# A hybrid encoder layer on one core: attention's tiles taken in another order, copies reordered, and half of the first output unit's products placed in the last head

## What is computed

```python
q = (_rms(c_q, norm_q[l]) @ w_uq[l]).reshape(B, L, N_HEADS, NOPE_DIM + ROPE_DIM)
kv = (_rms(c_kv, norm_kv[l]) @ w_ukv[l]).reshape(B, L, N_HEADS, NOPE_DIM + V_DIM)
s = (einsum('bqhd,bkhd->bhqk', q_n, k_n) + einsum('bqhr,bkr->bhqk', q_r, k_r))
p = softmax(s * scale)          # over the keys of one sequence
attn = einsum('bhqk,bkhd->bqhd', p, v).reshape(B, L, N_HEADS * V_DIM) @ w_o_attn[l]
```

## Time and profile before

| | |
|---|---|
| median of 3 runs | 1320.33 us (1320.19 to 1321.05) |
| the profiled execution's own time | 1321.35 us |
| its span | 1319.6 us |
| TensorE busy | 1281.5 us (97%), 7181 matmuls |
| VectorE busy | 689.2 us (52%) |
| ScalarE busy | 466.1 us (35%) |
| GpSimd busy | 328.7 us (25%) |
| chain that ended last | PE 87%, DVE 5%, ACT 4%, issue 3% |
| attention, 361 to 571 us | TensorE busy 195.62 of 210.00 us, VectorE 159.83, ScalarE 134.27, GpSimd 87.04 |

### The profile page before, as it was taken

The page is one execution under the profiler, slowest core; times in us unless marked ns, Lnnn a source line. Parts: engine busy times, 40 slices in busy tenths (PEclk is TensorE's granted clock), DMA queues, the critical chain, the costliest instruction groups (busy, mean ns, idle before and its releaser), DMA issues.

```text
span 1319.6 us, 18184 instructions
## 1 busy us (share of the span) xinstructions
PE 1281.5 (97%) x7181; PEld 1109.9 (84%) x7181; DVE 689.2 (52%) x781; ACT 466.1 (35%) x689; POOL 328.7 (25%) x198
## 2 busy tenths in 40 slices
PE   6999999999999999989999999999999999999996
PEld 4888888888888888878888888888888888888885
DVE  4699999998768788773732131111111233343334
ACT  6211123422266666643522242222222333333325
POOL 2000000000034344426322222222222222233333
PEclk9999999999999999999999999999999999999998
DMA  6221222443210011033352212222222111111112
GB/s 193 70 63 52 61 73 65 122 116 101 76 41 22 21 33 47 17 95 100 111 207 78 64 48 65 64 64 64 64 63 64 62 67 64 64 64 64 64 48 96
DMA packets 123938, 96.18 MB, mean 73 GB/s; under 512 B 9725, under 2 KB 106043, under 8 KB 123882
## 3 DMA queue, kind: packets, MB, share of 16 engines
q1 hardware_dynamic: 121392, 88.96, 22.6%
q10 hardware_dynamic: 2490, 6.45, 1.4%
HBM read 85.96 MB, written 9.44 MB: 72 GB/s over the span
## 4 chain that ended last, share of the span: by engine, by line
PE 87%; DVE 5%; ACT 4%; issue 3%; ACTq 0%; POOL 0%; DVEq 0%
PE psum L319 56%; PE psum L1642 24%; PE psum L1519 3%; DVE acc L945 2%; PE psum L1549 1%; PE psum L1402 1%; PE psum L1531 1%; ACT junk L828 1%; PE psum L1367 1%; ACT prob L611 1%; ACT pthi L618 1%; DVE ptlo L1030 0%; PE psum L1484 0%; ACT uhi L511 0%; PE psum L1649 0%
## 5 line engine op out<-in xcount | busy, mean ns | idle before, releaser
L303 POOL TENSOR_TENSOR wlo<-raw,whi 128x1024 fp32r<-128x1024 f32 (+1 forms) x105 | 240.7, 2292 | 860.9 <-ACT whi L298 860.9
L298 ACT ACTIVATE whi<-raw 128x1024 fp32r<-128x1024 f32 (+2 forms) x144 | 146.9, 1020 | 470.0 <-PE psum L319 255.1
L945 DVE SCALAR_TENSOR_TENSOR acc<-cs,convw,acc 128x799 f32<-128x799 f32 x232 | 244.2, 1117 | 0.0
L1221 DVE TENSOR_TENSOR hidlo<-hid,hidhi 128x1536 fp32r<-128x1536 f32 x32 | 82.1, 2566 | 169.8 <-ACT hidhi L806 169.8
L319 PE MATMUL psum<-uhi,wlo 128*128 128x512 f32 x592 | 152.7, 339 | 0.0
L319 PE MATMUL psum<-uhi,whi 128*128 128x512 f32 x592 | 152.2, 338 | 0.5 <-DVE wlo L303 0.5
L319 PE MATMUL psum<-ulo,whi 128*128 128x512 f32 x592 | 152.5, 339 | 0.0
L1642 PE MATMUL psum<-whi,hidhi 128*128 128x512 f32 x384 | 149.4, 389 | 0.0
L1642 PE MATMUL psum<-whi,hidlo 128*128 128x512 f32 x384 | 149.4, 389 | 0.0
L1642 PE MATMUL psum<-wlo,hidhi 128*128 128x512 f32 x384 | 149.4, 389 | 0.0
L1231 DVE SCALAR_TENSOR_TENSOR hid<-psum,rbc 128x768 f32 (+1 forms) x32 | 30.6, 958 | 216.6 <-PE psum L319 216.6
(11 more groups left out here) (223 smaller groups left out, 2063.7 us busy)
## 6 DMA issues: line engine op xcount, KB each, us to landing
raw<-in_w_in SPq DMA_DIRECT2D x38, 512.0 KB, 4.0
raw<-in_w_mlp_in SPq DMA_DIRECT2D x32, 512.0 KB, 4.1
raw<-in_w_mlp_out SPq DMA_DIRECT2D x32, 512.0 KB, 3.5
gates<-gout ACTq DMA_DIRECT2D x16, 384.0 KB, 2.4
gin<-gates SPq DMA_DIRECT2D x16, 384.0 KB, 3.1
raw<-in_w_o_attn SPq DMA_DIRECT2D x8, 512.0 KB, 3.9
raw<-in_w_conv_out SPq DMA_DIRECT2D x8, 512.0 KB, 3.8
raw<-in_w_out SPq DMA_DIRECT2D x8, 512.0 KB, 3.5
```

Of the source, the lines that this page charges most:

```text
L298: nc.scalar.activation(whi[:, c % 2, 0:w], raw[:, c % 4, 0:w], ACT.Copy).then_inc(hi_ready, 1)
L303: eng.tensor_tensor(out=wlo[:, c % 2, 0:w], in0=raw[:, c % 4, 0:w], in1=whi[:, c % 2, 0:w].bitcast(F32), op=ALU.subtract).then_inc(lo_read ...
L945: ins = nc.vector.scalar_tensor_tensor(out=a, in0=src, scalar=w, in1=a, op0=ALU.mult, op1=ALU.add)
L1221: nc.vector.tensor_tensor(out=hidlo[c % 2][:, :, :], in0=hid[:, ds(i * 8 + 2 * c, 2), :], in1=hidhi[c % 2][:, :, :].bitcast(F32), op=ALU.s ...
```

## The change

The tiles of a head are taken in the order given by Q_ORDER: position j = 0, 1 are the sample tiles, 2 to 5 the prompt tiles, and the outputs are written where they belong. So block 0 is the sample block and blocks 1 and 2 are prompt blocks. Around it:

- TensorE: A 0 stands ahead of T 3, and T 4 behind the first preparing product. The waits for the parts of queries and keys are spread over the products of a head's first score.
- ScalarE: the copies of block 1 (O 0, H_tails 1, H 3) stand ahead of E 5 instead of behind it; k_hi ahead of rotary_hi; in the odd head H 4 ahead of the rotary swap, H_tails 2, H 5 and O 1 behind q_hi, O 2 ahead of hi_unit 3.
- VectorE: four taps in each head of pairs 0 to 2 (before: three and five; in pair 0 two and six around the other steps), three in the final even head; L 4 behind them; k_lo inside the rotary sum.
- GpSimd: the additions stand between the divisions (in the even head in two halves behind the first and third, in the odd head behind the second); unit 4's split is moved from the even to the odd head, in two halves behind the third and fourth division; unit 5's stands ahead of the last division.
- The final odd head: ScalarE splits head 1 behind O(0, 2), heads 2 and 3 around E 5. VectorE splits 0 to 3 there. TensorE makes the products k = 0, 1 and k = 2, 3 of U_O's unit 0 around T 4; k = 4 to 7 follow after the head.

```diff
+Q_ORDER = (4, 5, 0, 1, 2, 3)
...
-            def start_pair(n, between=lambda step: None):
+            def start_pair(n, rest=None):
+                if rest is not None:
+                    H(rest, 1, 4)
                 rotary_swap(n)
-                between(0)
                 act.wait_ge(dup_landed[1], n * 16 + 32)
                 hi_unit(act, U_ATT, n, 2, W_V)
                 q_hi(n, 0, 1)
-                between(1)
+                if rest is not None:
+                    H_tails(rest, 1, 2), H(rest, 1, 5), O(rest, 1, 1)
+                k_hi(n, 0, 0)
                 rotary_hi(n)
-                k_hi(n, 0, 0)
+                if rest is not None:
+                    O(rest, 1, 2)
...
                     else:
                         E(p, hh, 0), E(p, hh, 1), O(p, 0, 2)
+                        if final:
+                            o_split_hi(1)
...
-                    H(p, hh, 0)
-                    H_tails(p, hh, 0), E(p, hh, 3), H(p, hh, 1)
+                    H(p, hh, 0), H_tails(p, hh, 0), E(p, hh, 3), H(p, hh, 1)
                     E(p, hh, 4), H(p, hh, 2)
+                    if hh == 1:
+                        if not final:
+                            act.wait_ge(kw_landed[0], p * 16 + 32)
+                        hi_unit(act, U_ATT, p, 5, D if final else W_QK)
+                        if final:
+                            o_split_hi(2)
+                    O(p, hh, 0), H_tails(p, hh, 1), H(p, hh, 3), E(p, hh, 5)
                     if hh == 0:
...
+                        q_hi(p, 1, 0), H(p, hh, 4), k_hi(p, 1, 1), H_tails(p, hh, 2), H(p, hh, 5), O(p, hh, 1)
+                        if final:
+                            o_split_hi(0)
+                    elif not final:
+                        start_pair(p + 1, p)
                     else:
...
-                    E(p, hh, 5), H_tails(p, hh, 1), H(p, hh, 3), O(p, hh, 0), H(p, hh, 4)
...
+                        o_split_hi(3), H(p, hh, 4), H_tails(p, hh, 2), H(p, hh, 5), O(p, hh, 1), O(p, hh, 2)
```

VectorE:

```diff
+                if rest is not None:
+                    L(rest, 1, 4)
                 rotary_cos(n)
...
+                q_lo(n, 0, 1)
+                if rest is not None:
+                    L_tails(rest, 1, 2), L(rest, 1, 5)
+                rotary_sum_lo(n, lambda step: k_lo(n, 0, 0))
                 v_lo_first(n)
...
                         M(p, hh, 0), M(p, hh, 1), R(p, hh, 0), R(p, hh, 1), M(p, hh, 2)
-                    R(p, hh, 2), M(p, hh, 3), L(p, hh, 0)
-                    L_tails(p, hh, 0), R(p, hh, 3), M(p, hh, 4), L(p, hh, 1)
-                    R(p, hh, 4), M(p, hh, 5), L(p, hh, 2)
+                        if final:
+                            o_split_lo(0)
+                    R(p, hh, 2), M(p, hh, 3), L(p, hh, 0), L_tails(p, hh, 0)
+                    M(p, hh, 4), R(p, hh, 3), L(p, hh, 1), R(p, hh, 4)
+                    L(p, hh, 2), M(p, hh, 5)
                     if final and hh == 1:
-                        o_split_lo(0)
-                    L_tails(p, hh, 1), R(p, hh, 5), L(p, hh, 3), L(p, hh, 4)
+                        o_split_lo(1)
+                    L_tails(p, hh, 1), L(p, hh, 3), R(p, hh, 5)
...
                     if hh == 0:
-                        q_lo(p, 1, 0), k_lo(p, 1, 1), L_tails(p, hh, 2), L(p, hh, 5)
...
+                        taps(0, 3 if final else 4)
+                        q_lo(p, 1, 0), L(p, hh, 4), k_lo(p, 1, 1), L_tails(p, hh, 2), L(p, hh, 5)
                     elif not final:
...
+                        taps(4, 8)
+                        start_pair(p + 1, p)
                     else:
-                        o_split_lo(1), L_tails(p, hh, 2), L(p, hh, 5)
-                        taps(2, 3)
+                        o_split_lo(2), o_split_lo(3), L(p, hh, 4), L_tails(p, hh, 2), L(p, hh, 5)
...
-            for h in range(2, HEADS):
+            for h in range(EARLY_HEADS, HEADS):
                 o_split_lo(h)
-                if 3 <= h < 6:
-                    tap(LAST, TAPS - 6 + h, LAST * TAPS + TAPS - 6 + h)
+                if h < HEADS - 1:
+                    tap(LAST, TAPS - 7 + h, LAST * TAPS + TAPS - 7 + h)
```

GpSimd (N is the division of a tile):

```diff
+                w4 = D if final else W_QR
+                N(0, 0), ln_add(p * 2, ((0, 384),)), N(0, 1), N(0, 2), ln_add(p * 2, ((384, 384),))
+                N(0, 3), N(0, 4), N(0, 5)
+                N(1, 0), N(1, 1)
+                if not final:
+                    ln_add(p * 2 + 1)
+                N(1, 2), lo_piece(p, 4, 0, w4 // 2, w4), N(1, 3), lo_piece(p, 4, w4 // 2, w4, w4)
+                N(1, 4)
+                lo_unit(gp, U_ATT, p, 5, D if final else W_QK)
+                N(1, 5)
```

TensorE:

```diff
                 for step, (a, b) in enumerate(ops):
+                    if q == 0 and step == 0:
+                        pe.wait_ge(qn_lo, p * 2 + (hh + 1))
+                        pe.wait_ge(kn_hi if hh == 1 else kn_lo, p * 2 + (hh + 1))
+                    if q == 0 and step == 1 and hh == 1:
+                        pe.wait_ge(kn_lo, p * 2 + (hh + 1))
+                    if q == 0 and step == 3 and hh == 0:
+                        pe.wait_ge(qr_lo, p + 1)
...
+            def first_outputs(ks):
+
+                pe.wait_ge(lo_ready, U_O + 1)
+                wh, wl = weights(0, KD)
+                for k in ks:
+                    pe.wait_ge(o_lo, k + 1)
+                    mm = products(psum[:, 0], (wh[:, k], wl[:, k]), o, k, ZSEG, k == 0, k == KD - 1)
+                if ks[-1] == KD - 1:
+                    mm.then_inc(unit_used, 1)
...
-                    T(p, hh, 3), A(p, hh, 0), T(p, hh, 4)
+                    A(p, hh, 0), T(p, hh, 3)
...
-                        T(p, hh, 5), A(p, hh, 1), A(p, hh, 2)
+                        pe.wait_ge(exp_ready, done + 5)
+                        first_outputs((0, 1)), T(p, hh, 4), first_outputs((2, 3)), T(p, hh, 5)
+                        A(p, hh, 1), A(p, hh, 2)
...
+                if m == 0:
+                    first_outputs(range(EARLY_HEADS, KD))
```

100 lines of the change are left out of this document (38 added, 62 removed).

## The result

The changed kernel takes 1310.99 us (median of 6 runs, 1309.88 to 1312.48); the kernel before, on the same chip, 1321.05 us (6 runs, 1320.19 to 1322.03). The ratio is 0.9924 with a 95% interval of 0.9912 to 0.9935: 10.06 us or 0.76% faster, where 3.25 us were forecast.

The account below looks back on a forecast made before the run. TensorE is busy nearly throughout, so only its idle time or lowered clock, near 20 us, can be won. Terms -1.25 + 1.4 - 6.45 + 2.15 + 0.9 = -3.25 us gave a 1317.1 us median; 8-in-10 range 1312.7 to 1320.9.

Parts of the forecast that it names:

- first score of pair 0: Pair 0's start: only the fourth product waits for the rotary low half, winning 1.25 us of a 1.6 us wait.
- even heads, pairs 0, 1, 2, 3: Even heads: short score waits and a late key low half behind the taps; sum +1.4 us.
- odd heads, pairs 0, 1, 2: Odd heads: moved copies and GpSimd pieces find cover; 28.4 us each, sum -6.45 us, the gain.
- last head and first unit: Last head's first score to the unit's end: 31.7 us for 28.8, +2.15 us without the moved block.
- clock: TensorE's clock may fall in the half-busy tail of the last head: +0.9 us taken, ends 0 and +1.7.
- Third, fourth and fifth score wait ... 1.05 us in all: Even heads: these scores wait about 0.26, 0.35 and 0.35 us behind ScalarE's copies, with 0.1 after.
- The next head waits about 0.6 us: End of even heads: knlo ready at 21.8 us behind four taps, so the odd head starts late.
- covered better: Rival, chance 0.25: no knlo wait in even heads (-2.5), short olo collision (-0.3), clock holds (-0.9); 1313.4 us.
- the filling: Last head: four output products brought forward gain nothing, as VectorE paces the second half of the unit.
- The slower rival: Rival, chance 0.1: GpSimd's pieces meet the even heads' taps, 1.66 us each for 1.04; 8.1 us more, 1325.2 us.
- the tail eats it: Rival, chance 0.25: last head costs more by worse order (+0.3), clock (+0.8), score waits (+1.8); 1320.0 us, no change.
- The clock alone holds: Case inside the forecast's range, no own chance: the tail keeps its clock; 1316.2 us.

Follow-up runs that it names:

- x10_taps_odd: Changed kernel with two taps in the even heads of pairs 0 to 2 and six in the odd ones, for four and four; 1309.64 us, ratio 0.9909.
- x4_waits_front: Changed kernel with all waits of a pair's first score put back ahead of its first product; 1311.53 us, ratio 0.9922.
- x7_gpsimd_back: Changed kernel with GpSimd's additions and split of unit 4 again behind the sixth division of each head; 1330.26 us, ratio 1.0068.
- x8: Kernel before with the new order of tiles alone, sample tiles first; 1320.01 us, ratio 0.9983.
- x12: Kernel before with GpSimd's new order alone, unit 5's split left behind the last division; 1316.45 us, ratio 0.9967.
- x3_exp_ahead: Changed kernel with the last exponential again ahead of the second block's copies; 1313.08 us, ratio 0.9928.
- x5_taps_even: Changed kernel with six taps in the even heads of pairs 0 to 2 and two in the odd ones; 1319.05 us, ratio 0.9976.
- x2_no_fill: Changed kernel with all eight products of the first output unit behind the last head; 1312.66 us, ratio 0.9928.
- experiment 8: Changed kernel with the first output unit's products all behind the last head (1312.66 us), then with output splits moved earlier instead (1306.84, 1304.55, with moved taps 1303.70 us).
- the early splits: Changed kernel with splits of heads 4 to 6 moved into the last head, 1306.84 us; heads 0 to 3 also earlier, 1304.55; taps two and six too, 1303.70.

## Why the prediction was wrong, step by step

The sum forecast, and the same terms read from the two traces (the 0.75 us that the order moves from even to odd heads taken out of both):

| term | forecast us | measured us |
|---|---|---|
| first score of pair 0 | -1.25 | -1.79 |
| even heads, pairs 0, 1, 2, 3 | +1.35, +0.35, +0.35, -0.65 | +0.48, -0.84, -1.06, -1.62 |
| odd heads, pairs 0, 1, 2 | -2.95, -2.1, -1.4 | -3.21, -2.05, -1.24 |
| last head and first unit | +2.15 | +1.01 |
| clock | +0.9 | with the line above |
| sum | -3.25 | -10.32 |

The measured lengths come from the starts of the heads' first scores: 370.73, 392.68, 420.82, 441.40, 469.85, 490.24, 518.79 and 539.05 us after; 373.08, 395.30, 425.90, 448.07, 477.82, 500.02, 529.06 and 551.69 before.

**The step that failed is the even heads**: +1.4 forecast, -3.0 measured, 4.4 of the 7.1 us. (Some of the wait for knlo now stands in the odd heads; even and odd heads together were forecast at -5.05 and measured at -9.54, 4.5 us apart, wherever that wait is counted.) The pieces of TensorE were right: 10.9 us to the queries and 9.2 behind them, against 9.03 measured in pair 1, and a whole head of 20.26 us in pair 3. What was wrong is everything that was put on top. "Third, fourth and fifth score wait ... 1.05 us in all": they wait 0.33 us in pair 3 and 0.65 in pair 1. The ready times had been made by adding the shown durations of neighbours on ScalarE and VectorE, while their starts lie closer, 1.73 us for 2.01 in the rows above; that this is the whole difference was not tried apart. "The next head waits about 0.6 us" for knlo, "near 2 for pair 0": the wait is 0.5 us by x10_taps_odd, in pair 0 too, and it stands behind the first product of the odd head's first score, so the even head carries almost none of it. And the taps, "14.35 to 19.2", took 14.26 to 18.65, as the division among them was held up by the taps and not they by it. Each error is a few tenths and all have one sign, and they come four times. A forecast made of ready times some tenths apart from the need should have had the small waits as a term with two ends, one of them zero, in every head.

The rival *covered better* named just this ("VectorE's queue runs ahead of my reckoning"), took 2.5 us for it and had 0.25 of the chance. Its three conditions came about in the main, the mechanism was right, and the size was little more than half: 1313.4 for 1311.0. The same error sits in it, for it removed only the knlo waits and left the 1.05 us of each head.

**Right: the odd heads**, to 0.05 us in sum, and that the gain is there at all because copies find cover and GpSimd leaves the taps alone. Partly by luck: without a wait for knlo they last 27.97 us by x10_taps_odd, less than the 28.05 of pieces and 0.35 of waits reckoned, and the wait for knlo, which the forecast had at the end of the even head, now lies inside the odd head's first score.

**Right in kind, off in size: the last head.** All waits came in the forecast order, the collision of olo and wlo went the short way (olo 1.05 us, wlo 3.09 for 2.38), and the filling, forecast to gain nothing, gained 0.6 us, by the clock. The first two products were forecast to about a tenth (k 0 starts at 10.32 us for 10.45, k 1 at 11.77 for 11.7); then k 3 ended at 17.1 for 18.3, as the exponential ahead of olo 2 came 0.65 us sooner and the two low halves took 2.19 us together. I read that 1.2 us as durations added on two engines again; no run tests it.

**Wrong in size: the clock.** It did not fall in the traced execution of the changed kernel. Where it fell in others with the same tail, it fell inside the paced part and cost 0.14 us at most (below), the low end that the forecast had named and not taken.

**Half right: the first score.** -1.79 for -1.25, but 0.88 of it came back as waits inside the same head, and x4_waits_front shows that spreading the waits was worth 0.2 us over the whole stretch.

**The slower rival** (GpSimd meets the taps) did not come about, and x7_gpsimd_back shows that it was real and under-priced: 18.2 us, not 8.1, since it was reckoned for the even heads only, without the weights that come late in the odd ones and the clock that falls behind the waits. The rival *the tail eats it* did not come about either: the tail lasted less than reckoned. *The clock alone holds* gave 1316.2; the clock held in the traced execution, but the heads brought more.

What stays open: x8 and x12 alone give 2.6 and 4.3 us. The other 3.4 us of the stretch are shared by the order of copies on ScalarE and VectorE, the placing of taps, and what these make of each other; only the last exponential's place (1.0), the filling (0.5) and the waits (0.2) were measured apart, and their sum leaves some 1.7 us to parts that weren't tried alone. That the parts add is itself not shown.

## What to carry to other kernels

When the question is whether a copy is ready some tenths before it is asked for, build the ready times from the starts of instructions that follow each other in the trace, not from their durations, and carry "no wait" as one end of every such term. When work is moved on one engine, look at what it meets on its neighbour: here the same additions and weight split of GpSimd took 18.2 us more behind the divisions, beside VectorE's taps, than between them. Look for a fallen clock before you give such a price to one cause. And products brought forward into a gap gain little while the operands behind them are made at the old pace: 0.6 us here, all of it because TensorE's clock stayed up, while moving the operands' copies gained 4.8.

## What the runs showed of the hardware

In these runs the clock fell or did not fall after the same work. The last head of x10_taps_odd is that of the changed kernel, 1.9 us earlier. TensorE's busy time in aligned stretches of 2 us, first the changed kernel:

```profile
555.00:557.00 2.00, 2.00 (x16) 1.00 0.00 0
557.00:559.00 2.00, 1.44 (x13) 1.00 0.00 0
559.00:561.00 2.00, 1.75 (x13) 1.00 0.00 0
561.00:563.00 2.00, 0.00 (x0) 1.00 0.00 0
563.00:565.00 2.00, 1.50 (x7) 1.00 0.00 0
```

and x10_taps_odd:

```profile
553.10:555.10 2.00, 2.00 (x16) 1.00 0.00 0
555.10:557.10 2.00, 1.44 (x13) 1.00 0.00 0
557.10:559.10 2.00, 1.74 (x13) 1.00 0.00 0
559.10:561.10 2.00, 0.00 (x0) 1.00 0.00 0
561.10:563.10 2.00, 1.97 (x7) 0.59 0.00 0
```

The same products, the same idle 2 us, and then a granted clock of 0.59 in the one (the lower level for most of it) and 1.00 in the other. It cost nothing: the last head and the unit took 30.53 us for 30.55, since the slow products lay where VectorE's pace would have made TensorE wait anyway. The clock also fell in the tails of x3_exp_ahead, x4_waits_front and x5_taps_even, at 30.65, 30.58 and 30.69 us. In x2_no_fill it fell earlier, after 0.49 us of work in 4.64, on products that nothing paced, and there it cost the 1.6 us of experiment 8. With the early splits, where no such gap is left, the clock stayed at 1.00 in all three kernels. The Trainium skill (TensorE: Matmul & The Clock Gate, Part 1) says of the rise at a kernel's start that its point varies with when the work falls, not with the work alone; no run here shows that rise, but the two traces agree for the fall.
